# Hybrid decoder trunk: expert weights loaded in another order, a tenth place for them in the last layer, and the second gather moved between the halves of gate and up

## The reference

```
lg = xf @ w_rg + b_rg ; grp = argmax(lg)                  # one of 4 groups
le = (xf @ w_re + b_re) of that group                      # 8 experts in it
top_p, top_e = top_k(softmax(le), 2)                       # two experts a token
gu = ragged_dot(xs, w_gu, sizes)                           # 1024 -> 1024: gate and up
ys = ragged_dot(silu(g_) * u_, w_dn, sizes)                # 512 -> 1024: down
h  = h + sum over a token's two experts of gate * ys
```

## Time and profile before

| | |
|---|---|
| median of 3 runs | 1406.6 us (1403.84 to 1411.74) |
| the profiled execution, its own time | 1408.52 us |
| its span in the trace | 1406.5 us |
| TensorE busy | 1235.7 us, 88% of the span |
| VectorE, ScalarE, GpSimd busy | 490.9, 245.7, 77.0 us |
| bytes moved by DMA | 455.24 MB, 324 GB/s over the span |
| mean granted TensorE clock | 0.958 |

### The profile page before, as it was taken

The page is one execution under the profiler, slowest core; times in us unless marked ns, Lnnn a source line. Parts: engine busy times, 40 slices in busy tenths (PEclk is TensorE's granted clock), DMA queues, the critical chain, the costliest instruction groups (busy, mean ns, idle before and its releaser), DMA issues.

```text
span 1406.5 us, 26131 instructions
## 1 busy us (share of the span) xinstructions
PE 1235.7 (88%) x10688; PEld 736.2 (52%) x10688; DVE 490.9 (35%) x1094; ACT 245.7 (17%) x569; POOL 77.0 (5%) x104
## 2 busy tenths in 40 slices
PE   7989997997899888888899889979988998889886
PEld 6867665544444444344488766654434543344333
DVE  5265525432232222222343553363222232222233
ACT  3012214111111111111210221231111111111111
POOL 1220300010000000000031121000000000000000
PEclk9999998999999999999999999989999999999998
DMA  8321339699899999999944013569998999999994
GB/s 350 138 109 61 120 119 419 256 429 427 383 411 427 431 426 431 426 431 427 428 160 155 31 61 120 244 294 380 430 426 367 429 430 427 430 427 430 427 430 204
DMA packets 33263, 455.24 MB, mean 324 GB/s; under 512 B 3776, under 2 KB 4160, under 8 KB 5312
## 3 DMA queue, kind: packets, MB, share of 16 engines
q1 hardware_dynamic: 33216, 454.59, 77.1%
HBM read 453.53 MB, written 1.05 MB: 323 GB/s over the span
## 4 chain that ended last, share of the span: by engine, by line
PE 50%; DMA 40%; DVE 5%; issue 2%; ACT 2%; SPq 1%; DVEq 0%; ACTq 0%
PE bank L473 48%; DMA share<-in_w_gu 30%; DMA share<-in_w_dn 9%; SPq L378 1%; DVE small L1529 1%; PE bank L532 1%; PE bank L703 1%; DVE share L1509 1%; DVE rest L1822 0%; DMA share<-in_mem 0%; ACT xnT L1074 0%; ACT ring L1143 0%; DVE h L1445 0%; ACT xnT L1143 0%; PE bank L481 0%
## 5 line engine op out<-in xcount | busy, mean ns | idle before, releaser
L473 PE MATMUL bank<-share,rest 128*32 128x512 f32 (+1 forms) x2560 | 309.6, 533 | 17.8 <-DMA share<-in_w_dn 17.8
L473 PE MATMUL bank<-dense,rest 128*32 128x256 f32 (+2 forms) x1824 | 194.6, 485 | 28.2 <-DMA share<-in_w_gu 26.5
L473 PE MATMUL bank<-ring,rest 128*32 128x256 f32 (+1 forms) x1792 | 176.3, 479 | 24.4 <-DMA share<-in_w_gu 22.6
L473 PEld LDWEIGHTS bank<-share,rest 128*32 128x32 f32 x2560 | 102.5, 113 | 114.3 <-issue 97.2
L473 PE MATMUL bank<-xnT,dense 128*128 128x256 f32 (+2 forms) x928 | 153.3, 340 | 6.8 <-ACT xnT L1074 4.5
L473 PE MATMUL bank<-rest 96*128 96x512 f32 (+1 forms) x288 | 122.0, 579 | 34.3 <-DVE rest L1822 34.3
L473 PEld LDWEIGHTS bank<-dense,rest 128*32 128x32 f32 (+1 forms) x1824 | 70.4, 113 | 153.3 <-issue 99.1
L473 PEld LDWEIGHTS bank<-xnT,dense 128*128 128x128 f32 (+1 forms) x928 | 132.8, 177 | 23.6 <-issue 6.2
L473 PE MATMUL bank<-rest,xhat 128*128 128x96 f32 x1088 | 141.0, 284 | 2.6 <-DVE rest L1731 2.6
L1813 DVE TENSOR_TENSOR rest<-rest,bank 64x512 f32<-64x512 f32 x64 | 35.7, 558 | 301.3 <-ACT rest L1227 275.0
L473 PEld LDWEIGHTS bank<-rest,xhat 128*128 128x128 f32 x1088 | 130.2, 196 | 18.0 <-issue 15.9
(11 more groups left out here) (234 smaller groups left out, 961.3 us busy)
## 6 DMA issues: line engine op xcount, KB each, us to landing
share<-in_w_dn SPq DMA_DIRECT2D x64, 2048.0 KB, 19.8
ring<-in_w_gu SPq DMA_DIRECT2D x48, 2048.0 KB, 23.9
dense<-in_w_gu SPq DMA_DIRECT2D x48, 2048.0 KB, 25.9
share<-in_w_gu SPq DMA_DIRECT2D x32, 2048.0 KB, 23.1
dense<-in_w_units SPq DMA_DIRECT2D x18, 2048.0 KB, 9.5
dense<-in_w_units SPq DMA_DIRECT2D x4, 1024.0 KB, 6.2
dense<-in_w_units SPq DMA_DIRECT2D x2, 1184.0 KB, 5.7
ring<-in_w_units SPq DMA_DIRECT2D x2, 1024.0 KB, 14.1
```

Of the source, the lines that this page charges most:

```text
L473: return pe.matmul(out_ap, lhsT=lhsT, rhs=rhs, start=start, stop=stop, skip_group_check=True)
```

## The change

It has three parts.

1. **Order of the loads.** The first 12 turns are written out, and a table `LEADS` says for each layer and turn at which of five places slots 5 and 4 stand: lead 4 is at the very end of the turn, lead 0 at its start. In the first layer the table goes 3 (four turns), 2 (four), 1 (four), in the last layer 4, 3, 2, 1 (three turns each). The turns behind the twelfth have lead 0.
2. **A tenth place.** `memT` and `xnT` become the two halves of one tensor `streams` of 16 KB a partition. In the last layer, where neither is needed once the router has read `xnT`, slot 3 of odd pairs goes there. Slot 3 of pair 1 is then issued ahead of the turns, and in each turn slot 3 is loaded for pair t + 1 and not for pair t, behind slot 2. The final gain moves from `memT` to the head of `share`.
3. **The second gather.** `gather(t + 1, 1)` behind the transposes goes, and `gather(t, 1)` stands between the first product of the first half and the product of the further block. `gathered` is split: bank 1 of pair t is drained at the head of VectorE's turn t, bank 0 of pair t + 1 where both were.

```diff
-STEPS_AHEAD = 4
+STEPS_AHEAD = 12
+LEADS = [[3] * 4 + [2] * 4 + [1] * 4, [4] * 3 + [3] * 3 + [2] * 3 + [1] * 3]
...
-        memT = sb("memT", [P, 8, 256])
-        xnT = sb("xnT", [P, 8, 256])
+        streams = sb("streams", [P, 2, 2048])
...
-        gain_row = memT[:, :, :].rearrange("p k t -> p (k t)")[:, 0:D]
+        gain_row = share[:, 0:D]
...
+        def last_odd_slot(s):
+
+            return streams[:, :, :].rearrange("p s c -> p (s c)") if s == 3 else odd_slot(s)
...
+                ahead = int(odd_apart(l, 3))
+                if ahead:
+                    sp.wait_ge(ev("memG_ring"), l)
+                    bank_full(sp, l, "rt")
+                    alone(sp)
+                    load_of(3, 3, True)
...
                 def other_rows(t, odd, it):
 
                     sp.wait_ge(efilled[2], it)
                     alone(sp)
-                    load_expert(t % PAIRS, 3, odd)
+                    load_expert((t + ahead) % PAIRS, 3, odd != (ahead == 1))
...
+                def turn(t, odd, it, lead):
+
+                    if lead == 0:
+                        if not ahead:
+                            other_rows(t, odd, it)
+                        down(t, odd, it)
+                    small_rows(t, odd, it)
+                    if lead == 1:
+                        if not ahead:
+                            other_rows(t, odd, it)
+                        down(t, odd, it)
+                    large_rows(t, odd, it)
+                    if lead >= 2 and not ahead:
+                        other_rows(t, odd, it)
+                    if lead == 2:
+                        down(t, odd, it)
+                    large_other_rows(t, odd, it)
+                    if lead == 3:
+                        down(t, odd, it)
+                    if ahead:
+                        other_rows(t, odd, it)
+                    if lead == 4:
+                        down(t, odd, it)
+
                 for t in range(1, 1 + STEPS_AHEAD):
...
+                    turn(t, t % 2 == 1, t, LEADS[l][t - 1])
...
                     for b in range(2):
-                        pe.wait_ge(edrained[b], t + 2)
                         pe.wait_ge(edrained[2 + b], it * 2 + 1)
                     for half in range(2):
+                        pe.wait_ge(edrained[half], t + 2)
...
                         ins.then_inc(small_read if half == 0 else efilled[2], 1)
+                        if half == 0:
+                            gather(t, 1)
...
                     ins.then_inc(efilled[6], 1)
-                    gather(t + 1, 1)
...
                 with dve.Fori(0, npass * PAIRS) as t:
                     it = t
 
+                    gathered(t, 1)
                     dve.wait_ge(onehot_ready, t + 1)
...
-                    gathered(t + 1)
+                    gathered(t + 1, 0)
```

More of the change, by code:

```diff
@@ L101, in hymba @@
         h = sb("h", [P, 2, 1024])
-        memT = sb("memT", [P, 8, 256])
-        xnT = sb("xnT", [P, 8, 256])
+        streams = sb("streams", [P, 2, 2048])
+        memT = streams[:, 0, :].rearrange("p (k t) -> p k t", k=8)
+        xnT = streams[:, 1, :].rearrange("p (k t) -> p k t", k=8)
         xhat = sb("xhat", [P, 2, 1024])
@@ L247, in odd_slot, with odd_of, odd_apart @@
             return dense[:, s, :] if s < 3 else eslot(s)
+        def last_odd_slot(s):
+            return streams[:, :, :].rearrange("p s c -> p (s c)") if s == 3 else odd_slot(s)
+        def odd_of(l):
+            return last_odd_slot if l == DEPTH - 1 else odd_slot
+        def odd_apart(l, s):
+            return s < 3 or l == DEPTH - 1 and s == 3
         filled = [sem(f"bank{b}_filled") for b in range(8)]
@@ L255, in hymba @@
         eloaded_of = [[sem(f"expert{s}_loaded_{l}") for s in range(6)] for l in range(DEPTH)]
-        odd_loaded_of = [[sem(f"odd_expert{s}_loaded_{l}") for s in range(3)] for l in range(DEPTH)]
+        odd_loaded_of = [[sem(f"odd_expert{s}_loaded_{l}") for s in range(3 + l)] for l in range(DEPTH)]
         vloaded = sem("memory_value_weights_loaded")
@@ L339, in expert_loaded @@
         def expert_loaded(eng, l, t, odd, s):
-            if s >= 3:
+            if not odd_apart(l, s):
                 eng.wait_ge(eloaded_of[l][s], t * 16 + 16)
@@ L373, in load_of @@
                 def load_of(e, s, odd=False):
-                    dst, src = expert_dmas(l, e, s, odd_slot if odd else eslot)
-                    sp.dma_start(dst, src).then_inc(odd_loaded[s] if odd and s < 3 else eloaded[s], 16)
+                    dst, src = expert_dmas(l, e, s, odd_of(l) if odd else eslot)
+                    sp.dma_start(dst, src).then_inc(odd_loaded[s] if odd and odd_apart(l, s) else eloaded[s], 16)
                 def load_expert(pair, s, odd):
@@ L414, in first_rows, with large_rows @@
                     load_expert((t + 1) % PAIRS, 1, not odd)
+                def large_rows(t, odd, it):
                     sp.wait_ge(half_read, it)
@@ L417, in first_rows, with large_other_rows @@
                     load_expert((t + 1) % PAIRS, 0, not odd)
+                def large_other_rows(t, odd, it):
+                    sp.wait_ge(efilled[3], it)
+                    alone(sp)
+                    load_expert((t + 1) % PAIRS, 2, not odd)
                 def other_rows(t, odd, it):
@@ L431, in down @@
                     load_expert(t % PAIRS, 4, odd)
-                for t in range(1, 1 + STEPS_AHEAD):
-                    odd = t % 2 == 1
-                    first_rows(t, odd, t)
-                    other_rows(t, odd, t)
-                    sp.wait_ge(efilled[3], t)
-                    alone(sp)
-                    load_expert(t + 1, 2, not odd)
-                    down(t, odd, t)
+                def turn(t, odd, it, lead):
[20 more added lines that the diff above has]
+                        down(t, odd, it)
+                for t in range(1, 1 + STEPS_AHEAD):
+                    turn(t, t % 2 == 1, t, LEADS[l][t - 1])
                 odd_reg = sp.alloc_register(f"sp_odd_pair_{l}")
@@ L446, in _ @@
                         t, odd = i * 2 + step, step == 1
-                        other_rows(t, odd, t)
-                        down(t, odd, t)
-                        first_rows(t, odd, t)
-                        sp.wait_ge(efilled[3], t)
-                        alone(sp)
-                        load_expert((t + 1) % PAIRS, 2, not odd)
+                        turn(t, odd, t, 0)
                     sp.reg_add(odd_reg, odd_reg, 2)
                 it = sp.snap(odd_reg, min_val=1, max_val=MAXP * PAIRS)
-                other_rows(PAIRS - 1, True, it)
+                if not ahead:
+                    other_rows(PAIRS - 1, True, it)
                 down(PAIRS - 1, True, it)
@@ L943, in _ @@
                 gather(0, 0)
-                gather(0, 1)
                 wait("npass_ready")
@@ L1025, in _ @@
                     pair(i * 2, False, eslot)
-                    pair(i * 2 + 1, True, odd_slot)
+                    pair(i * 2 + 1, True, odd_of(l))
                 n_pairs = npass * PAIRS
@@ L1769, in _, with gathered @@
                 own("npass_ready", V.tensor_copy(npass_i[0:1, 0:1], r_np[0:1, :]))
[L1770 to L1777 removed]
+                def gathered(n, b):
+                    dve.wait_ge(efilled[b], n + 1)
+                    g = bc(pcol(l, G_FFN + 4 * b, 4).unsqueeze(2), 4, ROWS)
+                    V.tensor_tensor(xg[:, 4 * b:4 * b + 4, :], banks[b][:, 0:4 * ROWS].rearrange("p (d s) -> p d s", d=4),
+                                    g, MUL).then_inc(edrained[b], 1)
+                gathered(0, 0)
                 wait("route_exp")
```

11 lines of the change are left out of this document (2 added, 9 removed).

## The result

The changed kernel takes 1397.27 us in the median of 13 executions (1393.98 to 1401.91), the kernel before 1411.6 (1403.84 to 1413.36) in 13 beside it. The ratio is 0.9917, with a 95% interval of 0.9902 to 0.9932: faster, by 11.7 us of 1406.6. (The ratio compares the means, 1398.3 and 1410.1. The two medians lie further apart, since the executions of the kernel before fall into two groups.) The forecast was faster by 17.8, to about 1390. Executions of one kernel lie 8 to 10 us apart, so it takes the stages of the trace to say where the missing 6 us went.

The account below looks back on a forecast made before the run. The prediction took the experts' 2 MB transfers, 4.89 us each, to bound the kernel. Layer 0's -6.35 and layer 1's -11.43 made -17.8 us, giving 1390; the sum alone ranged 1386 to 1394, and 1384 to 1398 held somewhat over 8 in 10.

Parts of the forecast that it names:

- both gaps: Where the order of the turns changes in each layer's experts; new load order closes them: -4.18 and -4.37 us.
- about 7: Head of layer 1: after the streams transfer, an idle stretch of about 7 us where there were 14.
- The other price of the tenth place: Layer 1's head: 6.8 us by the skill's DMA fit, instead of 4.89; sum -19.7, near 1388.
- The 5.4 and 0.9 us in hand at the switches: Spare time before the queue runs dry: 5.4 for turn 5's down rows, 0.9 for layer 1's third transfer.
- the rival that the gap moves: At a new switch or layer 1's third transfer the queue runs dry again: 4 us a layer back, 1398; chance 0.12.
- the one that the hole eats the tenth place: Layer 1's head: a hole behind the added transfer takes its 4.89 us gain, giving 1395; chance 0.05.
- The term -1.97 a layer for the start: Each layer's start: pair 0 waits for one gather only, so it and the first free place come 1.97 us earlier.
- the rival that the start gives nothing: Each layer's start: slow clock lengthens pair 0's first product; +1.97 to +3.4 us a layer, 1394 to 1397; chance 0.12.
- the gather alone fills the time up to 251.1: Layer 0's start: argument against the start rival, since the clock had been at half rate until about 251.7.
- The price of 0 for the straight code: SyncE's written-out turns: no cost in the sum; slower by the code or something unseen had chance 0.04.
- The -0.2 a layer for the tail: Each layer's end: the gather for a pair 16 falls away, so the last down product begins 0.2 us sooner.
- TensorE's pair at 25.9: Each later pair: ScalarE's copy stands open some 0.75 us, so TensorE takes 25.9, 3.4 under the transfers; cost 0.

Follow-up runs that it names:

- e_pad: Changed kernel with 60 idle instructions a turn meant for SyncE; they are not in the program that ran, so it is the changed kernel again; ratio 0.993.
- e_tenth: Kernel before plus the tenth place alone, with four turns written out, old order and gathers as before; ratio to the kernel before 1.0012.
- e_best: Changed kernel with 6 turns written out in place of 12 and eight spare products ahead of the down product in each pair; ratio to before 0.9934.
- e_fill4: Changed kernel with eight spare products between the first gather and pair 0, filling TensorE's pause at a layer's start; ratio to before 0.9934.
- e_straight: Kernel before with 12 turns of SyncE written out in the old order, nine places, gathers as before; ratio to before 1.0042.
- e_code: Changed kernel with ten spare register loads in each written-out SyncE turn behind the fourth; ratio to before 0.9956.
- e_short_new: Changed kernel with 6 turns written out in place of 12, keeping the new gather; ratio to before 0.9912.
- e_short: Changed kernel with 6 turns written out in place of 12 and the gathers as before; ratio to before 0.9939.

## Why the forecast was right in direction and too large

**The mechanism and both gaps: right.** No dip behind the first reload, the streams transfer issued at 930.70 and landing at 941.96, the hole at layer 1's head 10.52 between landings where it was 13.95. (The forecast said about 7 for it; the start, below, is what is missing, and in e_pad the hole was 9.30.) The other price of the tenth place did not come: it would be 6.8 us by the fit in the Trainium skill (DMA: Bandwidth & Descriptors, Anatomy of one DMA), which is given for transfers that GpSimd issues, while SyncE issues these, and 3.2 to 4.7 were measured. The 5.4 and 0.9 us in hand at the switches were enough: the rival that the gap moves, and the one that the hole eats the tenth place, did not come. With the old order the first of them comes (e_tenth), and with the short table and a slower TensorE too (e_best).

**The term -1.97 a layer for the start: wrong.** The step read "pair 0 begins 1.97 earlier, near 252.15, and the first place comes free 1.97 earlier". The first half held (252.08), the second didn't follow: the product began before the clock was up, and took 6.3 and not 3.4. This is the rival that the start gives nothing, with the price given there (the reload up to 1.4 later than before; measured -0.5 and +1.0), and I had given it 0.12. The weight was set by the remark that the gather alone fills the time up to 251.1. It does, at the lower level, and the clock was not yet up when it ended. e_fill4 shows the cause in layer 0. Cost: 1.5 and 3.0. The 3.0 is that of one execution; in e_pad, the same program, layer 1 lost 1.4 by it.

**The price of 0 for the straight code: wrong.** The forecast asked whether a fetch stalls SyncE, found the issues on time and looked no further. The issues are on time behind a fetch too, since the other 15 DMA engines keep their times. The cost is on the other side: a fetch puts one DMA engine back by 0.7, and once that engine is the last of the 16, every landing. That came twice a layer in full in the changed kernel. Turns 1 to 4 did not show it in the landings: the fetch at 362.00 stands in a full queue, but another engine was later. Cost 1.6 in layer 0 by the count of 63 transfers and about 1.4 in layer 1; e_straight measures it alone at 1.36 and 1.97.

**The -0.2 a layer for the tail: wrong in sign in this execution.** Without the gather ahead of it the last down product waits idle, and took 7.06 for 5.37 (layer 0) or began 1.07 late (layer 1). From the last landing to the end of that product are 7.33 (691.20 + 7.06 - 690.93) and not 5.6, and behind layer 1's last landing come 21.56 and not 20.73. Against -0.2 each that is 1.9 and 1.0 too much. The sign is no law: in the twelve layers with nothing ahead of that product, from the last landing to its end are 5.41 to 7.34 (5.61 before), and in two of them (layer 1 of e_code and of e_short_new) it is just the 0.2 less that the forecast said.

From a layer's first issue to the end of its last down product, layer 0 got -1.36: 691.20 + 7.06 - 200.81 = 497.45 now, 693.00 + 5.37 - 199.56 = 498.81 before. The forecast was -6.35, and 1.5 + 1.6 + 1.9 = 5.0 is the difference. Layer 1 with what lies behind it got -6.41 + 0.83 = -5.58 for -11.43; 3.0 + 1.4 + 1.0 = 5.4 of the 5.85 between them are accounted for, 0.4 are not. The two come to -6.9 for -17.8. What the ratio has beyond that lies in the mixing stages, which the change touches only in when they begin, and there this trace can't be told from chance. The three terms come from single executions, and the start and the tail scatter by as much as 1.6 and 1.9 from one to the next: the sum closes here partly because the same trace gives both its sides.

**TensorE's pair at 25.9: a little low.** It takes 26.2 to 26.3 in the changed kernel, with the copy open for 0.9, still 3.1 under the transfers, and costs nothing.

**Open.** Why the clock rises 4.4 us behind the gather in one layer and 10.8 in the other of the same run (e_fill4), and why the same pause ahead of the last down product slows it in one execution and not in the next; no experiment took that apart. The stage between the layers takes from 196.24 (e_best) to 203.10 us (e_short); the longer ones have more stretches at the lower clock, but that was not tried. Why a packet that takes 0.31 us puts its engine back by 0.7 the traces do not show.

## What to carry to other kernels

When a step is moved forward, price the step at the clock that it will meet: a product that begins before the clock is up takes up to 6.5 us for 3.6, one behind an idle end up to 7.1 for 5.4, and that can take what the move gave. A queue that runs ahead needs its next release sooner as well, so an added place pays only together with the order that closes the next gap. And code that is written out to tune such an order costs transfers where the queue is full: write out as few turns as the order needs, and measure the code by itself, with the order left as it was.

## What the runs showed of the hardware

- A fetch of one 8 KB packet of SyncE's instructions beside a full queue of 2 MB transfers puts one of the 16 DMA engines back by about 0.7 us until the queue next runs empty. Landings move only when that engine is the last: by 0.69 to 0.74 then (once 0.83), by 0.1 to 0.7 at the fetch that makes it the last, and not at all before. One fetch comes about every 130 instructions of SyncE in straight code, and none in the loop.
- The lags add up: the last transfer's first and last engine are 3.57 and 3.74 us apart in the changed kernel, 0.64 and 1.03 in the kernel before, 5.18 and 5.07 in e_code.
- Eight spare f32 products a pair (2.0 us; 23 us more of TensorE in 428) left the transfers as full as they were, and the clock stood at 1.00 where it had been 0.98. The same products in layer 1's start, at the lower level, had the first reload at 61.36 in place of 60.01, in one execution.
- A pause of 1.6 to 2.0 us of TensorE ahead of the last down product, in stages whose mean clock was 0.97 to 0.98, was followed by a product at the lower level in six of ten cases (7.06 us for 5.37). With work in the pause it never was, in 16.
